# Sample scores of a hybrid decoder step: two samples stacked on 128 partitions, four matmuls in place of eight

## The reference, cut to what matters

```python
N_HEADS = 16; N_KV_HEADS = 4; D_HEAD = 64; DEC_BATCH = 8; DEC_SEQ = 4; PAST_LEN = 256
k_all = concatenate([k_past, k], axis=1)              # 256 cached keys and 4 new ones
score = where(causal, score, -inf)                    # the indexer's scores
_, idx = lax.top_k(score, k_sel)                      # which keys a query may see
s = einsum('btngd,btjnd->btngj', q, k_g) * D_HEAD ** -0.5
p = softmax(s); o = einsum('btngj,btjnd->btngd', p, v_g)
```

## Time and profile before

| | before |
|---|---|
| three runs, us | 1539.98, 1539.63, 1539.28 |
| profiled execution, its own time, us | 1539.3 |
| its span, us, and granted clock | 1537.5, 0.999 |
| busy: PE, PEld, DVE, ACT, POOL, us | 1526.7, 1510.1, 1023.9, 666.3, 461.6 |
| DMA | 282.16 MB, mean 184 GB/s |
| sample scores (L787): matmul records, in four groups | 64, of 16 each |
| their starts, us | 398.8 to 499.1 |

### The profile page before, as it was taken

How to read it: one execution, slowest core, us unless ns; L and a number is a source line. 1 busy time by engine, 2 the same in 40 slices (tenths; PEclk the granted TensorE clock), 3 DMA queues, 4 the chain that set the end, 5 groups by cost and what they waited for, 6 DMA issues and landing times.

```text
span 1537.5 us, 33758 instructions
## 1 busy us (share of the span) xinstructions
PE 1526.7 (99%) x12448; PEld 1510.1 (98%) x12448; DVE 1023.9 (67%) x1477; ACT 666.3 (43%) x901; POOL 461.6 (30%) x581
## 2 busy tenths in 40 slices
PE   8999999999999999999999999999999999999998
PEld 8999999999999999999999999999999999999998
DVE  7655789888666676567676767777777764444443
ACT  7344345554666644444333333333333333333332
POOL 8992468877422101221111111111111100001100
PEclk9999999999999999999999999999999999999999
DMA  8886477776866586565554545454545475555552
GB/s 269 240 206 186 143 215 205 205 209 194 247 206 200 156 206 209 166 217 173 160 172 156 176 152 177 150 178 149 181 148 183 146 225 176 174 174 173 168 179 94
DMA packets 300222, 282.16 MB, mean 184 GB/s; under 512 B 35280, under 2 KB 292832, under 8 KB 300000
## 3 DMA queue, kind: packets, MB, share of 16 engines
q1 hardware_dynamic: 283968, 256.70, 55.8%
q10 hardware_dynamic: 13840, 16.62, 3.5%
q0 software_dynamic: 2320, 7.54, 1.6%
HBM read 266.73 MB, written 14.05 MB: 183 GB/s over the span
## 4 chain that ended last, share of the span: by engine, by line
PE 88%; DVE 0%; ACT 0%; issue 0%
PE banks L579 28%; PE banks L581 28%; PE banks L580 28%; PE banks L589 1%; PE banks L774 0%; PE banks L815 0%; PE banks L724 0%; PE banks L787 0%; PE banks L711 0%; PE banks L828 0%; PE banks L733 0%; PE banks L636 0%; PE banks L830 0%; DVE wlo L1325 0%; PE banks L900 0%; DVE t L1518 0%
## 5 line engine op out<-in xcount | busy, mean ns | idle before, releaser
L1325 DVE TENSOR_TENSOR wlo<-raw,whi 128x1024 fp32r<-128x1024 f32 x443 | 558.1, 1272 | 285.7 <-ACT whi L953 279.8
L953 ACT ACTIVATE whi<-raw 128x1024 fp32r<-128x1024 f32 x443 | 462.3, 1051 | 546.5 <-PE banks L581 494.6
L581 PE MATMUL banks<-h_hi,wlo 128*128 128x288 f32 x1408 | 415.7, 295 | 0.0
L580 PE MATMUL banks<-h_lo,whi 128*128 128x288 f32 x1408 | 415.7, 295 | 0.0
L579 PE MATMUL banks<-h_hi,whi 128*128 128x288 f32 x1408 | 414.6, 294 | 0.0
L579 PE MATMUL banks<-hhi,whi 128*128 128x288 f32 (+1 forms) x912 | 271.5, 298 | 2.7 <-DVE hlo L1351 2.4
L581 PE MATMUL banks<-hhi,wlo 128*128 128x288 f32 (+1 forms) x912 | 269.0, 295 | 0.0
L580 PE MATMUL banks<-hlo,whi 128*128 128x288 f32 (+1 forms) x912 | 268.9, 295 | 0.0
L580 PEld LDWEIGHTS banks<-h_lo,whi 128*128 128x128 f32 x1408 | 264.6, 188 | 0.1
L581 PEld LDWEIGHTS banks<-h_hi,wlo 128*128 128x128 f32 x1408 | 264.4, 188 | 0.0
L579 PEld LDWEIGHTS banks<-h_hi,whi 128*128 128x128 f32 x1408 | 264.1, 188 | 0.1
(11 more groups left out here) (354 smaller groups left out, 2162.1 us busy)
## 6 DMA issues: line engine op xcount, KB each, us to landing
raw<-in_w_up SPq DMA_DIRECT2D x352, 256.0 KB, 3.4
raw<-in_w_in SPq DMA_DIRECT2D x223, 256.0 KB, 3.4
raw<-in_w_down SPq DMA_DIRECT2D x176, 256.0 KB, 3.0
raw<-in_w_glu SPq DMA_DIRECT2D x64, 256.0 KB, 3.2
raw<-in_w_out SPq DMA_DIRECT2D x64, 256.0 KB, 3.3
raw<-in_w_attn_proj SPq DMA_DIRECT2D x32, 256.0 KB, 4.1
scratch_gates<-gt ACTq DMA_DIRECT2D x16, 288.0 KB, 4.2
gbt<-scratch_gates POOLq DMA_DIRECT2D x8, 288.0 KB, 3.7
```

The source lines that it names most:

```text
L580: pe.matmul(out, h, xl[:, kt, :], start=False, stop=False)
L581: mm = pe.matmul(out, lo, xh[:, kt, :], start=False, stop=kt == nk - 1)
L953: act.activation(whi[:, s, :, 0:cols], raw[:, s, :, 0:cols], ACT.Copy).then_inc(hi_ready, 1)
L1325: dve.tensor_tensor(wlo[:, s, :, 0:cols], raw[:, s, :, 0:cols], whi[:, s, :, 0:cols], ALU.subtract).then_inc(lo_ready, 1)
```

## The change

The partitions are now shared out by sample, not by head: the tensor `kst[n]` holds for head n the keys of the pair's first sample on partitions 0 to 63 and of its second on 64 to 127, and `qst` the queries likewise, with the other sample's columns zero. One matmul of 128 rows then does for head (p, n) what two of 64 rows did. Keys and queries of one head of one sample have to be brought to the right half: the page DMAs become two of 64 partitions each, and the POOL copies run on 64 partitions, half of them from one half to the other, each followed by a wait for its own end.

```diff
-    kTb = [at(f"kTb{i}", [P, NPR, SK], F32, (WK + 41088, GR)[i]) for i in range(2)]
-    qbs = at("qbs", [P, NPR, 2, 32], F32, WK + 43168)
+    kst = [at(f"kst{n}", [P, NPR, SK], F32, (WK + 41088, GR)[n]) for n in range(2)]
+    qst = at("qst", [P, NPR, 2, 32], F32, WK + 43168)
...
                     for g, page in enumerate(pages(2 * j + b)):
-                        sp.dma_start(kTb[b][:, :, P * g:P * (g + 1)], I["cache_k"][ds(page, 1)].rearrange("a (p q) s -> q (a p) s", p=NPR)
-                                     ).then_inc(sem("k_in"), 16)
+                        heads = I["cache_k"][ds(page, 1)].rearrange("a (p n d) s -> n d (a p) s", p=NPR, n=2)
+                        for n in range(2):
+                            sp.dma_start(kst[n][DH * b:DH * (b + 1), :, P * g:P * (g + 1)], heads[n]).then_inc(sem("k_in"), 16)
...
-                pe.wait_ge(sem("k_in"), 64 * j + 64)
-                pe.wait_ge(sem("new_ready"), 4 * j + 4)
+                pe.wait_ge(sem("k_in"), 128 * j + 128)
+                pe.wait_ge(sem("new_ready"), 8 * j + 8)
...
-                for b in range(2):
-                    for p in range(NPR):
-                        for n in range(2):
-                            r, h = slice(DH * n, DH * (n + 1)), 2 * p + n
-                            mm = pe.matmul(aux[32 * h:32 * h + 32, 3, 0:SK], qbs[r, p, b, :], kTb[b][r, p, :], start=b == 0, stop=b == 1)
+                for p in range(NPR):
+                    for n in range(2):
+                        h = 2 * p + n
+                        mm = pe.matmul(aux[32 * h:32 * h + 32, 3, 0:SK], qst[:, p, n, :], kst[n][:, p, :], start=True, stop=True)
...
-            def new_keys(i):
-
-                copy(kTb[i % 2][:, :, PAST:SK], kT[:, :, TP + DS * i:TP + DS * (i + 1)]).then_inc(sem("new_ready"), 1)
+            staged = [0]
+
+            def crossing(out, a, rows):
+
+                copy(out, a, ones[rows, 0:1]).then_inc(sem("new_ready"), 1)
+                staged[0] += 1
+                pool.wait_ge(sem("new_ready"), staged[0])
+
+            def new_keys(i, n):
+
+                b, r = i % 2, slice(DH * n, DH * (n + 1))
+                crossing(kst[n][DH * b:DH * (b + 1), :, PAST:SK], kT[r, :, TP + DS * i:TP + DS * (i + 1)], r)
...
+                pool.wait_ge(sem("unit_staged"), 4 * j if j else 2)
+                if j == 3:
+                    pool.wait_ge(sem("vs_ready"), 2)
                 for b in range(2):
                     i = 2 * j + b
-                    copy(qbs[:, :, b, :].rearrange("p a (g b t) -> p a g b t", g=4, b=2)[:, :, :, b, :],
-                         qT[:, :, TP + DS * i:TP + DS * (i + 1)].rearrange("p (a g) t -> p a g t", a=2)).then_inc(sem("new_ready"), 1)
-                    if i != 1:
-                        new_keys(i)
+                    for n in range(2):
+                        r = slice(DH * n, DH * (n + 1))
+                        crossing(qst[DH * b:DH * (b + 1), :, n, :].rearrange("p a (g b t) -> p a g b t", g=4, b=2)[:, :, :, b, :],
+                                 qT[r, :, TP + DS * i:TP + DS * (i + 1)].rearrange("p (a g) t -> p a g t", a=2), r)
+                        if n == 0 or j:
+                            new_keys(i, n)
...
-            new_keys(1)
+            new_keys(0, 1)
+            new_keys(1, 1)
             z_out(pool, NUT - 1)
```

More of the change, by code:

```diff
@@ L1874, in copy @@
             def copy(out, a, by=None):
-                one = ones[:, 0:1] if by is None else by
+                one = ones[0:out.shape[0], 0:1] if by is None else by
                 for k in range(len(out.shape) - 2):
@@ L2104, in _ @@
                     stage_prompt(0)
-                    own.link(pool.memset(qbs[:, :, :, :], 0.0))
+                    own.link(pool.memset(qst[:, :, :, :], 0.0))
                     stage_sample(0)
```

## The result

The changed kernel took 1544.78 us, median of 7 runs (1542.79 to 1549.1), where the kernel before took 1539.63 (7 runs, 1539.28 to 1539.98): ratio 1.0035, 95% interval 1.0025 to 1.0044. It is slower by 5.15 us, clear of the 0.2% that a measurement can tell. The forecast was 1538.1, and its range ended at 1540.1. The profiled execution took 1544.25, with a span of 1542.4, so 4.9 more than before's 1537.5.

What follows compares the result with a forecast made beforehand. The prediction took PE's own sequence as the bound. Its terms, -1.76 (scores) + 0.1 (unit 0) + 0.1 (unit 1) = -1.56 us, from the median 1539.63 gave 1538.1 us, with a range of 1537.3 to 1540.1.

Steps and rivals of the forecast that it cites:

- What PE saves: At the scores (L787), two matmul waves fewer a pair, 0.44 us each for four pairs: 1.76 us saved.
- What SP's queue pays: On SP, four more key DMAs a pair at 0.56 us from one to the next: 2.24 us a pair.
- D: Extra time a pair's key DMAs hold SP's queue: taken as 2.24 us, with 5.1 as the upper bound.
- Unit 0: GLU stage, unit 0: the second chunk's later load delays the last state tile; PE is charged 0.1 us.
- 2.03 us of cover: Unit 0: the part of D absorbed before DVE takes PE's gate result; 0.21 us pass on.
- Unit 1: GLU stage, unit 1: the third chunk's later load moves ACT's start by 0.5 us; PE is charged 0.1 us.
- The room of 0.47: Unit 1: slack in us before PE would wait for `o_rows`, after coming 0.44 earlier by pair 0's saving.
- given back: Rival: unit 1's third chunk lands 2.24 us later, PE waits 1.77, the saving goes; 1539.7 us, chance 0.23 (wholly or mostly).
- POOL: Eight staging copies a pair instead of four, at most 3 us more, covered by POOL's waits: nothing charged.
- Gained in full: On PE's sequence: any piece that gets shorter is gained whole, unless PE then waits for something just in time today.
- SP dear: Rival: half-height key DMAs cost SP 5.1 us a pair, delaying chunks in units 0 and 1; 1542.5 us, chance 0.08.
- The Trainium skill's advice: On the key DMAs: use one transfer of 128 partitions, since two disjoint halves share engines and go one after the other.

## Why the prediction was wrong

**What PE saves: right.** Pair 1's scores in the kernel after, in the timeline (compare):

```profile
435.72 0.65 PE L787 MATMUL banks<-kst,qst 128*32 128x260 f32 x8
436.30 0.40 PE L580 MATMUL banks<-zhi,whi 128*128 128x288 f32 x1
```

0.58 us from first start to next chunk, forecast 0.57; 1.74 us in all, forecast 1.76. The tall tiles run side by side.

**What SP's queue pays: the first step that failed.** The prediction took "2.24, by the median" of the keys' own row, and called it D. D was 4.3. The line of the key DMAs in the kernel after (compare):

```profile
L484 SPq DMA_DIRECT2D kst<-in_cache_k x32: 598/604/1361, 383.6 to 477.1; - x32
```

All eight of a pair are dear, not only the four new ones: 8 x (0.60 + 0.18) = 6.2 against 4 x 0.56 = 2.2 is already 4.0. The trace of before had the price. SP's DMAs to 64 partitions (`lt`) and to 32 (the other two lines) take what the halves took, and the state tile's four in the earlier trace rows have a pitch of 0.65:

```profile
L319 SPq DMA_DIRECT2D lt<-scratch_flam_t x24: 547/594/617, 169.2 to 310.3; - x24
L341 SPq DMA_DIRECT2D zs<-scratch_z x28: 591/626/2620, 220.5 to 388.9; - x28
L458 SPq DMA_DIRECT2D tlag<-scratch_lag x32: 560/602/612, 186.1 to 380.2; - x32
```

The prediction was right that these keys on 64 partitions were not in the trace, but rows of other DMAs on as few partitions were, and they were nearer to the new one than the row of the DMA that it replaced. (The number of partitions is not the whole of it: the mask, spread over 128, took 0.56, and the new values, on 4, took 0.37, the median of L491.) The upper bound of 5.1 for D held, and the text's own price for it, 2.9 us in unit 0, was near the 2.4 that came.

**Unit 0: right path, wrong size.** The chain load, rounding, gate result, sigmoid, state tile is the one that made PE wait, and 2.03 us of cover was right: ACT took the chunk 4.91 late, DVE's gate result was 2.80 late, so 2.11 were covered. With D = 4.3 the working gives 404.65 for the end of the low part; it was 405.15, since the load landed 0.6 later than its issue moved.

**Unit 1: the direction right, the size too small.** ACT's start moves by less than the issue of the load: 1.52 for 2.58 in the run with POOL's copies, 4.05 for 6.41 in the kernel after, about 0.6 for 1 and not the 0.5 for 2.24 that was taken. The room of 0.47 fits the one run that shows a wait here, the copies alone. Even with D = 2.24 some 0.9 would have been paid here, near the case called "given back". In the kernel after nothing was paid, because unit 0 had been.

**POOL: nearly nothing,** as forecast, but the cover named (waits for DVE) was not the only thing behind the copies: the mask's store stands there, and SP waits for it.

**"Gained in full": a third place on PE's path.** The prediction looked for places with little room and named two. The turn of `ps` in unit 0's middle has less than both, none beyond the 0.15 us of hand-over: with the matmuls alone all of pair 0's 0.44 was lost there, so that at most 1.3 us of the 1.76 were to be had without moving `ps` too. In the kernel after it doesn't show, since PE came late.

**Two terms were not in the sum at all.** The clock: after the wait PE ran at 1.2 GHz for 3.4 us, +1.6; a wait was priced at its own length. The Trainium skill, "TensorE: Matmul & The Clock Gate", section "HAM oscillation — how this bites in real kernels", describes the same: waits for data drop the engine to its lower clock, and the work behind them is done at half speed. The traces agree for the waits of 2.57 to 5.68 us in the GLU stage (after, the halves alone, pair 0's keys moved, the narrow matmuls), but not for the stops of 1.9 to 2.7 us at the down projection, which left the clock at 1.00. And what the shorter program does elsewhere, by the theory the instruction supply: the prediction said that "nothing else of the group goes away" and that a shorter PE sequence is gained in full; taking 64 instructions out moved every later instruction of PE, and one place some 750 to 850 us on cost 1.9 to 2.5 us, all that the matmuls save. The change of the order on PE was four rows, and no row there shows it.

**The terms together.** The profiled executions differ by +4.9 where -1.6 was forecast. Of the 6.5 us, 2.3 are the wait in unit 0 (2.44 for 0.1), 1.6 the clock and 2.5 the stop (nothing for either). With D right alone the sum would have been about +0.7, or 1540.3: the size of D is the step that failed first, but it is less than half of the miss.

**The rivals.** "SP dear" was the mechanism of the first term, with a chance of 0.08 and 1542.5; with the clock and the stop, which that rival did not have, it came to 1544.8. The halving of a transfer by partitions bought nothing by itself, and the run with the halves alone is 1.0028 (1.0018 to 1.0037). The Trainium skill's advice that the prediction weighed ("DMA: Bandwidth & Descriptors", "Rules for kernel authors") was right for this kernel; the price was in the issue, which the advice does not give as its reason.

## What to carry to other kernels

Price a new DMA by the rows of DMAs on as many partitions, not by the row of the DMA that it replaces (and by the dearest of them, since the number of partitions alone did not decide it here), and look at what stands behind it in its queue; put transfers that are needed late behind those that are needed next. When PE is the bound and waits, add to the wait what the clock may cost behind it. And in a program with thousands of instructions a saving of 2 us by taking some out can be lost where the program leaves a loop: look at the whole span for a new "issue" gap, and if there is one, try the same kernel with the count of instructions restored.

## What the runs showed of the hardware

- On SP a DMA of 128 partitions was issued in 0.37 us, one of 64 in 0.60, with 2 heads a partition or 4 (0.598/0.604 and 0.598/0.614 us lowest/median), one of 32 in 0.60 to 0.63; but the mask on 128 took 0.56 and the new values on 4 took 0.37. What it is in the form that costs was not taken apart.
- PE stood for 1.9 to 2.7 us, waiting for nothing that the trace shows, four matmuls behind the exit of a loop, with 64 instructions fewer or 192 more ahead of it, and not at all with the count as before. The packet of the instruction queue behind the one at this place came 3.5 to 5.5 us later in the kernels with the stop, 10.4 to 12.9 in those without.
- After waits of 2.57, 3.05 and 4.14 us in unit 0 the granted clock was 0.5 for 3.41 us; with 5.68 in unit 1 for 6.83, the first 1.5 of it before the wait ended; after 2.67 at the down projection it stayed 1.00. What tells these apart the runs do not show.
- Four matmuls of 32 columns of weights and 4 columns of data cost 0.06 us a pair (0.37 saved a pair with them, 0.44 without), about half of the 0.12 expected.
